# One-core transformer kernel: sums of squares as steps of their own, the latent product regrouped, its copies moved to VectorE, two-strip weight units in one transfer

## The chip, the cores and the metric

The kernel runs on 1 core of one Trainium2 chip. The metric is the device time in microseconds (us), the median of several runs. The engines are called PE (TensorE), DVE (VectorE), ACT (ScalarE), POOL (GpSimd) and SP (SyncE, which here issues nearly all transfers).

## The reference

Two transformer blocks run one after the other on x of 256 tokens by 1024 channels, in float32. The first has a differential attention and a neighbourhood attention beside it, then `x = x + rmsnorm(merged @ w_out)`, then a gated feed-forward part and `x = x + rmsnorm(f)`. The second block begins with a norm and one wide projection, of which these columns matter here:

```
u = rmsnorm_2(h, ln_mix[l])
z = u @ w_in[l]
c_q, c_kv, k_rope, g_q, g_k, g_v, g_lr, g_og, gate_a, gate_b = jnp.split(z, offsets, axis=-1)
...
mix = jax.nn.sigmoid(gate_a) * y_a + jax.nn.sigmoid(gate_b) * y_b
```

`y_a` is a latent attention: c_q (384 columns) and c_kv (256) each get a norm and a further projection (`uq`, `ukv`), k_rope (32) is rotated. `y_b` is a gated linear attention, whose decay comes from g_lr (16). After it come `h = h + mix @ w_out`, a second gated feed-forward part, and a last norm. Everything must come out in float32 accuracy.

## The kernel before, in words

Every large product is made of *strips*: 128 rows of the weight matrix against two token tiles t = 0 and t = 1 of 128 tokens each. To keep accuracy, each float32 operand is split into a high part (rounded by ACT) and a low part (the rest, by DVE), and a strip takes three passes on PE: high by high, high by low, low by high (`product`, line 1019). A strip of 1024 columns is six matmuls of 512 columns per tile. PE has to do all of this, so the other engines have to deliver in time:

- **Weights.** SP loads them into a ring of nine slots (`weights(u)`, line 576), waiting for the slot to be used up by t = 1. ACT splits off the high part (`advance` of the scalar block, line 656), DVE the low part (line 1284 with a gain column, line 1281 without). A planner gives each unit a due time; `advance(ahead_of(i, 2.2))` before each strip does all splits due within 2.2 strips. *Units* are one strip, except in `up5`, `up25` and `gla_qk`, whose narrow strips go two to a slot.
- **Activations.** They are turned (transposed) on PE (`turn`, line 965) into one of four PSUM banks `aux0` to `aux3`, split into high by ACT (`turned_high`, line 664) and low by DVE (line 1303). Before PE writes a bank again it waits for that bank's last reader (`into`).
- **Products** accumulate in `acc`, two banks per token tile. `take(name, t)` empties them; the next product on the same t waits for it (`acc_reader`).

`timeline()` writes one list of steps that every engine walks through in the same order, each doing its own share, and each engine's queue is in order: an instruction that waits holds all that stand behind it. `run(name, sizes, after)` goes through a product in groups of strips, first t = 0 and then t = 1 of each group; `after[t, kt]` are steps put behind strip kt of tile t. So the places that the change touches are:

- **out to up0**: after `take("out", 1)` ACT sums the squares of the result (line 669, tile `silu_tmp`), POOL makes the reciprocal root (lines 1725, 1726), DVE multiplies by the gain (line 1374, `row`) and adds into `x` (line 1381); then `norm_turn("ffn", 1)` turns `x` for the next product. `norm_turn` of the tags `ffn`, `mix2` and `ffn2` also has ACT sum the squares of `x` (`pre_norm`, line 669, tile `row`), and POOL make the root.
- **down to latent**: the same with `down`, `mix2` and `latent`.
- **latent to gla_qk**: `latent` has 688 columns (384 + 304: c_q, c_kv, k_rope, g_lr), in one group of eight strips. Its `take` has ACT copy g_lr out of PSUM (`gate_lr`, line 715) and square c_q and c_kv out of PSUM (line 669, tile `heads`); DVE then copies both to `row` (line 1404), each behind its square, and then k_rope (line 1407). `latent_turn` turns `row` for `uq` and `ukv`, `gate_lr_turn` turns g_lr, and `decay_logits`, two logistic passes on ACT and DVE, and `decay_sums` follow inside `gla_qk`.

## Time and profile before

| | |
|---|---|
| runs | 773.81, 774.9 and 1085.3 us, median 774.9 us |
| the profiled execution's own time | 774.11 us |
| its span | 772.4 us |
| mean granted TensorE clock | 0.999 of full speed (2.4 GHz) |
| PE busy | 760.7 us, 98% of the span |
| DVE, ACT, POOL busy | 473.5, 402.4, 55.8 us |
| moved | 134.34 MB, 174 GB/s in the mean |

The span runs from the first to the last instruction; 1.7 us of the execution's own time lie around it. PE's matmuls overlap and their ends are modelled, so the starts are what to go by: in steady running one 512-column matmul starts 0.23 us after the other.

### The profile page before, as it was taken

What the parts mean: (1) busy time and instruction counts of PE and PEld (TensorE: products, weight loads), DVE (VectorE), ACT (ScalarE), POOL (GpSimd) and SP (SyncE); (2) the same over time, 40 slices, a digit from 0 to 9 for tenths busy, and PEclk for the clock granted to TensorE, in tenths of its full rate; (3) what the DMA queues carried; (4) which work ended last, traced back from release to release, by engine and by line L of the source; (5) the groups of instructions that cost most, each with busy time, mean ns of one, the idle gap of its engine ahead of it and who ended that gap; (6) DMA issues with size and microseconds to landing.
All of it is one profiled execution on the core that took longest, in us unless ns stands there. A gap on an engine that the chain in (4) does not pass through costs nothing.

```text
span 772.4 us, 10412 instructions
## 1 busy us (share of the span) xinstructions
PE 760.7 (98%) x3974; PEld 632.6 (82%) x3974; DVE 473.5 (61%) x705; ACT 402.4 (52%) x599; POOL 55.8 (7%) x130
## 2 busy tenths in 40 slices
PE   8999999999999999999999999999999999999996
PEld 6887878888788888988887787888888888889885
DVE  5576756576855656765357796555765665666632
ACT  5646766444654535544367563666355454444421
POOL 1100100000450000000042000200001000000000
PEclk9999999999999999999999999999999999999999
DMA  8865353555655655654556374342555655564531
GB/s 309 262 190 210 119 191 113 185 161 177 214 170 189 214 161 171 216 165 162 157 173 220 96 227 128 109 162 84 191 170 161 215 180 172 193 205 147 194 136 56
DMA packets 57520, 134.34 MB, mean 174 GB/s; under 512 B 8135, under 2 KB 13438, under 8 KB 57470
## 3 DMA queue, kind: packets, MB, share of 16 engines
q1 hardware_dynamic: 56960, 132.34, 52.7%
q10 hardware_dynamic: 510, 1.33, 0.5%
q8 instruction: 32, 0.52, 0.3%
q14 instruction: 18, 0.15, 0.1%
HBM read 132.60 MB, written 1.05 MB: 173 GB/s over the span
## 4 chain that ended last, share of the span: by engine, by line
PE 95%; ACT 1%; DVE 1%; DMA 1%; issue 1%; POOL 1%; SPq 0%; POOLq 0%; DVEq 0%; ACTq 0%
PE acc L1019 84%; PE aux L965 4%; PE aux L1133 2%; PE aux L1082 1%; PE aux L1112 1%; DMA weights_raw<-in_w_in_dram 1%; PE aux L1205 1%; PE aux L1100 1%; DVE weights_low L1284 0%; PE aux L954 0%; ACT h_high L664 0%; PE aux L1243 0%; ACT row L669 0%; PE aux L1235 0%; ACT silu_tmp L669 0%
## 5 line engine op out<-in xcount | busy, mean ns | idle before, releaser
L1019 PE MATMUL acc<-weights_high,h_high 128*128 128x512 f32 (+2 forms) x752 | 232.7, 389 | 2.6 <-DVE k_rope L1407 1.6
L1284 DVE SCALAR_TENSOR_TENSOR weights_low<-weights_raw,gain_columns,weights_high 128x1024 fp32r<-128x1024 f32 (+3 forms) x189 | 219.2, 1192 | 14.8 <-ACT weights_high L656 13.9
L1019 PE MATMUL acc<-weights_high,h_low 128*128 128x512 f32 (+2 forms) x752 | 225.0, 379 | 0.0
L1019 PE MATMUL acc<-weights_low,h_high 128*128 128x512 f32 (+2 forms) x752 | 224.6, 378 | 0.4 <-DVE weights_low L1284 0.4
L656 ACT ACTIVATE weights_high<-weights_raw,gain_columns 128x1024 fp32r<-128x1024 f32 (+3 forms) x188 | 195.5, 1075 | 25.5 <-DMA weights_raw<-in_w_in_dram 14.7
L1019 PEld LDWEIGHTS acc<-weights_low,h_high 128*128 128x128 f32 x752 | 138.2, 188 | 28.2 <-DVE weights_low L1284 1.3
L1019 PEld LDWEIGHTS acc<-weights_high,h_low 128*128 128x128 f32 x752 | 138.3, 188 | 26.6
L1019 PEld LDWEIGHTS acc<-weights_high,h_high 128*128 128x128 f32 x752 | 133.1, 189 | 28.5 <-issue 4.5
L1281 DVE TENSOR_TENSOR weights_low<-weights_raw,weights_high 128x1024 fp32r<-128x1024 f32 x68 | 80.9, 1220 | 35.9 <-ACT weights_high L656 35.8
L656 ACT ACTIVATE weights_high<-weights_raw 128x1024 fp32r<-128x1024 f32 x68 | 69.4, 1056 | 47.8 <-DMA weights_raw<-in_ffn_w_down_dram 21.8
L1725 POOL TENSOR_SCALAR stats<-stats 128x1 f32<-128x1 f32 (+1 forms) x15 | 8.5, 568 | 625.5 <-ACT row L669 300.8
L1019 PE MATMUL acc<-weights_high,y_high 128*128 128x512 f32 (+1 forms) x148 | 46.6, 396 | 0.0
L1391 DVE SCALAR_TENSOR_TENSOR silu_tmp<-silu_tmp,acc 128x512 f32<-128x512 f32 (+1 forms) x24 | 15.4, 643 | 50.2 <-ACT silu_tmp L712 50.2
L712 ACT ACTIVATE silu_tmp<-acc,stats 128x512 f32<-128x512 f32 (+1 forms) x24 | 15.6, 649 | 58.5 <-PE acc L1019 58.5
L1019 PE MATMUL acc<-weights_high,y_low 128*128 128x512 f32 (+1 forms) x148 | 45.1, 386 | 0.0
L1019 PE MATMUL acc<-weights_low,y_high 128*128 128x512 f32 (+1 forms) x148 | 45.1, 386 | 0.0
L1019 PE MATMUL acc<-weights_high,f_high 128*128 128x512 f32 x112 | 36.1, 396 | 0.0
L1019 PE MATMUL acc<-weights_high,f_low 128*128 128x512 f32 x112 | 36.0, 395 | 0.0
L1019 PE MATMUL acc<-weights_low,f_high 128*128 128x512 f32 x112 | 36.0, 395 | 0.0
L1303 DVE SCALAR_TENSOR_TENSOR y_low<-aux,y_high 128x512 fp32r<-128x512 f32 (+1 forms) x20 | 12.8, 650 | 35.2 <-ACT y_high L664 35.2
L808 ACT ACTIVATE probs<-probs,stats 128x256 f32<-128x256 f32 (+1 forms) x48 | 23.1, 482 | 21.0 <-DVE stats L1515 21.0
L664 ACT ACTIVATE f_high<-aux 128x512 fp32r<-128x512 f32 (+1 forms) x16 | 8.7, 544 | 45.7 <-PE aux L965 45.7
(244 smaller groups left out, 678.0 us busy)
## 6 DMA issues: line engine op xcount, KB each, us to landing
weights_raw<-in_w_in_dram SPq DMA_DIRECT2D x55, 512.0 KB, 5.1
weights_raw<-in_w_down_dram SPq DMA_DIRECT2D x22, 512.0 KB, 4.6
weights_raw<-in_ffn_w_down_dram SPq DMA_DIRECT2D x22, 512.0 KB, 4.5
weights_raw<-in_w_gate_dram SPq DMA_DIRECT2D x40, 256.0 KB, 3.3
weights_raw<-in_w_up_dram SPq DMA_DIRECT2D x40, 256.0 KB, 4.0
weights_raw<-in_ffn_w_gate_dram SPq DMA_DIRECT2D x40, 256.0 KB, 3.4
weights_raw<-in_ffn_w_up_dram SPq DMA_DIRECT2D x40, 256.0 KB, 4.0
weights_raw<-in_w_out_dram SPq DMA_DIRECT2D x16, 512.0 KB, 4.7
```

Source lines behind the costliest of these rows:

```text
L656: nc.scalar.activation(hi[:, u % RING, d:d + w], raw[:, u % RING, d:d + w], ACT.Copy, scale=1.0 if g is None else gcol[:, g:g + 1])\
L664: nc.scalar.activation(dst[0][:, kt0:kt0 + n, t * P:(t + 1) * P], aux[bank][:, 0:n * P].rearrange("p (k s) -> p k s", k=n), ACT.Copy, scal ...
L712: nc.scalar.activation(fe[:, t, 0:w], a0[:, 0:w], ACT.Tanh, scale=stat(("half", (tag, t))))\
L808: j = nc.scalar.activation(T[:, i % 2, hb * 256:hb * 256 + n], T[:, i % 2, hb * 256:hb * 256 + n], ACT.Exp, scale=-1.0, bias=stat(("min", ...
L965: i = nc.tensor.transpose(aux[bank][0:w, n * P:(n + 1) * P], src, ident[:, :])
L1019: i = nc.tensor.matmul(acc[:, 2 * t + b, 0:width], lhs[:, k0, sl], w[:, u % RING, base + d:base + d + width], start=(kt == 0 and n == 0), ...
L1133: m = nc.tensor.matmul(aux[bank][:, d], probs_T[kind][:, i % 2, hb * 256 + kt * P:hb * 256 + (kt + 1) * P], v[:, kt, c], start=(kt == 0), ...
L1281: i = nc.vector.tensor_tensor(lo[:, u % RING, c], raw[:, u % RING, c], hi[:, u % RING, c].bitcast(F32), ALU.subtract)
L1284: i = nc.vector.scalar_tensor_tensor(lo[:, u % RING, c], raw[:, u % RING, c], gcol[:, g:g + 1], hi[:, u % RING, c].bitcast(F32), ALU.mult, ...
L1303: nc.vector.scalar_tensor_tensor(dst[1][:, kt0:kt0 + n, s], aux[bank][:, 0:n * P].rearrange("p (k s) -> p k s", k=n), scale, dst[0][:, kt0 ...
L1391: then(nc.vector.scalar_tensor_tensor(e, e, 1.0, a0[:, 0:w], ALU.add, ALU.mult))
L1725: then(g.tensor_scalar(ms, stat(("ss", key), width), 1.0 / n, EPS, ALU.mult, ALU.add))
```

## The change

Five things are done:

1. The squares of `x` (`pre_norm`) leave `norm_turn` and become steps `stats` of their own, on ACT and POOL: for `up0` and `up20` behind strips (0, 1) and (1, 0), for `latent` behind (0, 1) and (1, 1).
2. On ACT no weight is split at the last two strips of t = 1 of `out` and `down`, so that the squares of the result stand first once PE is done. `norm_turn("mix2", 0)` stands one strip earlier in `down`.
3. `latent` goes in groups of five and three strips. `norm_turn("mix2", 1)` stands behind strip 3 instead of 4. `latent_turn` 0 and 1 move into `gla_qk`, behind (0, 0) and (1, 0); `gate_lr_turn` 0 behind (1, 6), and 1 behind (0, 2).
4. DVE alone empties `latent`: one scaled copy of k_rope and g_lr together (48 columns, tile `k_rope_gate_lr`), then c_q and c_kv to `row`; ACT squares them out of `row` in SBUF instead of PSUM.
5. A unit of two strips comes in one transfer (two in `up5` and `up25`, one for each matrix) instead of two (four).

```diff
@@ timeline @@
     def ffn(up, down, tag, nxt):
-        run(f"{up}0", [4, 4], {(0, 2): [do("norm_turn", tag, 1)], (1, 7): [do("ffn_turn", f"{up}0", 0)]})
+        run(f"{up}0", [4, 4], {(0, 1): [do("stats", tag, 0)], (0, 2): [do("norm_turn", tag, 1)],
+                               (1, 0): [do("stats", tag, 1)], (1, 7): [do("ffn_turn", f"{up}0", 0)]})
...
         if nxt:
-            after[1, KF - 2] = [do("norm_turn", nxt, 0)]
+            after[1, KF - 3] = [do("norm_turn", nxt, 0)]
...
-    run("latent", [8], {(0, 4): [do("norm_turn", "mix2", 1)], (1, 3): [do("latent_turn", 0)],
-                        (1, 5): [do("gate_lr_turn", 0)]})
-    run("gla_qk", [4, 4], {(0, 3): [do("gate_lr_turn", 1)], (1, 2): [do("decay_logits")],
-                           (0, 5): [do("latent_turn", 1)], (1, 7): [do("decay_sums")]})
+    run("latent", [5, 3], {(0, 1): [do("stats", "mix2", 0)], (0, 3): [do("norm_turn", "mix2", 1)],
+                           (1, 1): [do("stats", "mix2", 1)], (1, 6): [do("gate_lr_turn", 0)]})
+    run("gla_qk", [4, 4], {(0, 0): [do("latent_turn", 0)], (0, 2): [do("gate_lr_turn", 1)],
+                           (1, 0): [do("latent_turn", 1)], (1, 2): [do("decay_logits")],
+                           (1, 7): [do("decay_sums")]})
@@ sync: weights(u) @@
+                n = PER.get(name, 1)
+                tile = raw[:, slot, 0:n * width_of(name)].rearrange("p (j w) -> p j w", j=n)
                 for m, kt, c, w, d in loads(u):
-                    src = dram[SC[name][1][m]][0, kt * P:(kt + 1) * P, c:c + w]
-                    sp.dma_start(raw[:, slot, d:d + w], src).then_inc(*tick(f"raw_loaded{slot}", u, 16))
+                    src = dram[SC[name][1][m]][0, kt * P:(kt + n) * P, c:c + w].rearrange("(j p) c -> p j c", p=P)
+                    dst = tile[:, :, d:d + w]
...
@@ scalar: take @@
                 elif name == "latent":
-                    nc.scalar.activation(lr[:, t, :], a1[:, 288:304], ACT.Copy, scale=scaled("mix2", t))\
-                        .then_inc(*tick("act", ("lr", t)))
+                    act.wait_ge(*at("acc_vec", ("latent", t)))
                     junk = ob2[:, t, :].bitcast(BF16)
-                    sum_squares(a0[:, 0:Q_RANK], junk[:, 0:Q_RANK], ("cq", t))
-                    sum_squares(a1[:, 0:KV_RANK], junk[:, Q_RANK:Q_RANK + KV_RANK], ("ckv", t))
+                    for key, c in (("cq", slice(0, Q_RANK)), ("ckv", slice(Q_RANK, Q_RANK + KV_RANK))):
+                        sum_squares(row[:, t, c], junk[:, c], (key, t))
@@ scalar: norm_turn, and the walk through the steps @@
-                    if tag in ("ffn", "mix2", "ffn2"):
-                        pre_norm(tag, t)
...
                 if st[0] == "mm":
+                    if st[1] in ("out", "down") and st[2] == TOKS - 1 and st[3] >= SC[st[1]][2] - 2:
+                        continue
                     advance(ahead_of(i, 0.8 if st[1] == "qk_a" else 2.2))
@@ tensor @@
-                    elif name == "latent":
-                        acc_reader[t] = [("acc_vec", (name, t)), ("act", ("lr", t))]
...
-                    pe.wait_ge(*at("act", ("lr", t)))
-                    turn(("lr", t), 2 + t, [lr[:, t, :]], ("turned_out", ("lr", t)))
+                    pe.wait_ge(*at("vec", ("lr", t)))
+                    turn(("lr", t), 2 + t, [klr[:, t, ROPE:ROPE + 16]], ("turned_out", ("lr", t)))
@@ vector: take @@
                 elif name == "latent":
+                    dve.wait_ge(*at("small2_loaded"))
+                    signal(nc.vector.tensor_scalar(klr[:, t, :], a1[:, KV_RANK:KV_RANK + ROPE + 16],
+                                                   scaled("mix2", t), None, ALU.mult), "vec", ("lr", t))
                     dve.wait_ge(*at("sumsq", ("mix2", t)))
-                    for s, src in ((slice(0, Q_RANK), a0[:, 0:Q_RANK]),
-                                   (slice(Q_RANK, Q_RANK + KV_RANK), a1[:, 0:KV_RANK])):
-                        if s.start:
-                            dve.wait_ge(*at("sumsq", ("ckv", t)))
-                        else:
-                            dve.wait_ge(*at("sumsq", ("cq", t)))
-                        i = nc.vector.tensor_copy(row[:, t, s], src)
...
+                    nc.vector.tensor_copy(row[:, t, 0:Q_RANK], a0[:, 0:Q_RANK])\
+                        .then_inc(*tick("acc_vec", (name, t)))
+                    nc.vector.tensor_copy(row[:, t, Q_RANK:Q_RANK + KV_RANK], a1[:, 0:KV_RANK])\
+                        .then_inc(*tick("acc_vec", (name, t)))
@@ gpsimd: the root for x @@
-                elif kind == "norm_turn":
-                    tag, t, *_ = a
+                elif kind == "stats":
+                    tag, t = a
                     if tag in ("ffn", "mix2", "ffn2"):
                         rstd("sumsq", (tag, t), D)
```

**ACT, from the end of `down` to the turns of the latent rows.** `silu_tmp,stats<-acc` are the squares of the result of `down`, `row,stats<-x` those of `x`, `heads_2` those of c_q and c_kv, `128x688` the splits of the weights of `latent`. Before:

```order
L656 ACTIVATE weights_high<-weights_raw,gain_columns 128x688 x3
L669 ACTIVATE silu_tmp,stats<-acc 128x1024
L656 ACTIVATE weights_high<-weights_raw,gain_columns 128x688 x3
L664 ACTIVATE h_high<-aux0 128x4x128
L664 ACTIVATE h_high<-aux1 128x4x128
L669 ACTIVATE row,stats<-x 128x1024
L656 ACTIVATE weights_high<-weights_raw,gain_columns 128x688
L669 ACTIVATE silu_tmp,stats<-acc 128x1024
L656 ACTIVATE weights_high<-weights_raw,gain_columns 128x688
L664 ACTIVATE h_high<-aux2 128x4x128
L664 ACTIVATE h_high<-aux3 128x4x128
L669 ACTIVATE row,stats<-x 128x1024
```

and now:

```order
L662 ACTIVATE weights_high<-weights_raw,gain_columns 128x688 x2
L675 ACTIVATE silu_tmp,stats<-acc 128x1024
L662 ACTIVATE weights_high<-weights_raw,gain_columns 128x688 x2
L670 ACTIVATE h_high<-aux0 128x4x128
L670 ACTIVATE h_high<-aux1 128x4x128
L675 ACTIVATE silu_tmp,stats<-acc 128x1024
L662 ACTIVATE weights_high<-weights_raw,gain_columns 128x688 x2
L675 ACTIVATE row,stats<-x 128x1024
L662 ACTIVATE weights_high<-weights_raw,gain_columns 128x688 x2
L670 ACTIVATE h_high<-aux2 128x4x128
L670 ACTIVATE h_high<-aux3 128x4x128
```

Two splits have moved from ahead of the first turned halves to behind the second squares of `down`, and `row,stats<-x` has moved behind them; four splits now stand between those squares and the halves of t = 1 (`aux2`, `aux3`).

**DVE, around the two `take`s of `latent`.** `L1404` (now also `L1406`) are the copies of c_q and c_kv to `row`, `128x512` the low parts of the weights of `gla_qk`. Before:

```order
L1404 COPY row<-acc 128x384
L1404 COPY row<-acc 128x256
L1407 TENSOR_SCALAR k_rope<-acc,stats 128x32
L1284 SCALAR_TENSOR_TENSOR weights_low<-weights_raw,gain_columns,weights_high 128x512 x2
L1303 SCALAR_TENSOR_TENSOR y_low<-aux0,y_high 128x4x128
L1303 SCALAR_TENSOR_TENSOR y_low<-aux1,y_high 128x128
L1284 SCALAR_TENSOR_TENSOR weights_low<-weights_raw,gain_columns,weights_high 128x512 x4
L1404 COPY row<-acc 128x384
L1404 COPY row<-acc 128x256
L1407 TENSOR_SCALAR k_rope<-acc,stats 128x32
```

and now:

```order
L1287 SCALAR_TENSOR_TENSOR weights_low<-weights_raw,gain_columns,weights_high 128x688 x2
L1287 SCALAR_TENSOR_TENSOR weights_low<-weights_raw,gain_columns,weights_high 128x512 x4
L1401 TENSOR_SCALAR k_rope_gate_lr<-acc,stats 128x48
L1404 COPY row<-acc 128x384
L1406 COPY row<-acc 128x256
L1287 SCALAR_TENSOR_TENSOR weights_low<-weights_raw,gain_columns,weights_high 128x512 x2
L1401 TENSOR_SCALAR k_rope_gate_lr<-acc,stats 128x48
L1404 COPY row<-acc 128x384
L1406 COPY row<-acc 128x256
```

The copies of t = 1 stood behind four narrow splits and the low parts of the first latent turn; now two narrow splits stand ahead of them, and the low parts come after.

**ACT in `gla_qk`**, from the second squares of c_q and c_kv to the first table load, now:

```order
L675 ACTIVATE heads_2,stats<-row 128x384
L675 ACTIVATE heads_2,stats<-row 128x256
L670 ACTIVATE y_high<-aux0 128x4x128
L670 ACTIVATE y_high<-aux1 128x128
L662 ACTIVATE weights_high<-weights_raw,gain_columns 128x1024
L866 ACTIVATE gate_lr_T<-aux3 16x128
L670 ACTIVATE y_high<-aux2 128x4x128
L670 ACTIVATE y_high<-aux3 128x128
L662 ACTIVATE weights_high<-weights_raw,gain_columns 128x1024
L871 ACT_TABLE_LOAD
```

The turned halves of t = 0 (`y_high`, `aux0` and `aux1`) stood ahead of these squares before; now they stand behind, and the copy of the turned g_lr of t = 1 (`gate_lr_T<-aux3`) behind them and one 1024-column split.

## Rows read from the trace of the kernel before

**Rows 1.** Page, part 1: busy time, share of the span, instructions.

```profile
PE 760.7 (98%) x3974; PEld 632.6 (82%) x3974; DVE 473.5 (61%) x705; ACT 402.4 (52%) x599; POOL 55.8 (7%) x130
```

**Rows 2.** Waits of PE: engine, line, released by: us in total, times, longest.

```profile
PE acc L1019 <- DVE k_rope L1407: 1.6, 1, 1.6
PE aux L965 <- DVE x L1381: 0.7, 2, 0.4
PE acc L1019 <- DVE weights_low L1284: 0.4, 1, 0.4
```

**Rows 3.** Timeline at out to up0: start, us, engine, line, tiles, count [idle before <-releaser].

```profile
195.19 1.03 PE L965 MATMUL aux<-ident,x 128*128 128x128 f32 x8
...
195.98 0.72 PE L1019 MATMUL acc<-weights_high,h_high 128*128 128x512 f32 x2
...
196.80 1.06 ACT L669 ACTIVATE row<-x 128x1024 f32<-128x1024 f32 x1
...
197.84 1.02 ACT L669 ACTIVATE silu_tmp<-acc 128x1024 bf16<-128x1024 f32 x1
...
198.83 2.20 ACT L656 ACTIVATE weights_high<-weights_raw,gain_columns 128x1024 fp32r<-128x1024 f32 x2
...
201.23 1.41 DVE L1381 SCALAR_TENSOR_TENSOR x<-row,stats,x 128x512 f32<-128x512 f32 x2 [0.93 <-POOL stats L1726]
...
202.04 1.32 PE L965 MATMUL aux<-ident,x 128*128 128x128 f32 x8 [0.31 <-DVE x L1381]
```

**Rows 4.** Timeline at down to latent.

```profile
385.82 0.87 ACT L656 ACTIVATE weights_high<-weights_raw,gain_columns 128x688 fp32r<-128x688 f32 x1 [1.29 <-DMA weights_raw<-in_w_in_dram]
...
386.27 0.63 PE L1019 MATMUL acc<-weights_low,f_high 128*128 128x512 f32 x2
386.60 1.06 ACT L664 ACTIVATE h_high<-aux 128x512 fp32r<-128x512 f32 x2
...
387.27 0.55 PE L1019 MATMUL acc<-weights_high,h_high 128*128 128x384 f32 x2 [0.37 <-issue]
...
388.59 0.87 ACT L656 ACTIVATE weights_high<-weights_raw,gain_columns 128x688 fp32r<-128x688 f32 x1
...
389.36 1.02 ACT L669 ACTIVATE silu_tmp<-acc 128x1024 bf16<-128x1024 f32 x1
...
390.25 0.47 PE L1019 MATMUL acc<-weights_high,h_high 128*128 128x384 f32 x2
...
392.67 1.32 PE L965 MATMUL aux<-ident,x 128*128 128x128 f32 x8 [0.39 <-DVE x L1381]
```

**Rows 5.** Timeline at latent to gla_qk.

```profile
401.81 2.73 ACT L656 ACTIVATE weights_high<-weights_raw,gain_columns 128x512 fp32r<-128x512 f32 x4 [3.87 <-DMA weights_raw<-in_w_in_dram]
...
407.68 0.27 PE L965 MATMUL aux<-ident,gate_lr 128*16 128x128 f32 x1
...
408.50 0.88 DVE L1404 COPY row<-acc 128x384 f32<-128x384 f32 x2
...
409.30 0.24 DVE L1407 TENSOR_SCALAR k_rope<-acc,stats 128x32 f32<-128x32 f32 x1
...
409.59 0.50 PE L1019 MATMUL acc<-weights_high,h_high 128*128 128x512 f32 x1 [1.65 <-DVE k_rope L1407]
...
409.94 0.40 PE L1019 MATMUL acc<-weights_high,h_low 128*128 128x512 f32 x1
...
410.18 0.40 PE L1019 MATMUL acc<-weights_low,h_high 128*128 128x512 f32 x1
...
417.12 0.69 DVE L1584 SCALAR_TENSOR_TENSOR log_decay<-log_decay,level_decay 128x512 f32<-128x512 f32 x1 [2.65 <-ACT level_decay L871]
...
419.82 1.05 PE L1180 MATMUL aux<-sum_up_to,log_decay 128*128 128x128 f32 x8
```

**Rows 6.** DMA issues: tensor, queue, count, KB each, median us to landing.

```profile
weights_raw<-in_w_in_dram SPq DMA_DIRECT2D x55, 512.0 KB, 5.1
...
gates<-in_rpb_dram SPq DMA_DIRECT2D x2, 438.0 KB, 12.1
```

More of the change, by code:

```diff
@@ L143, in loads @@
     out = []
-    for k, base, _ in strips(u):
-        for m, c, w, d in sorted(SC[name][3], key=lambda p: p[3]):
-            if out and out[-1][0] == m and out[-1][1] == k and out[-1][2] + out[-1][3] == c:
-                out[-1][3] += w
-            else:
-                out.append([m, k, c, w, base + d])
+    for m, c, w, d in sorted(SC[name][3], key=lambda p: p[3]):
+        if out and out[-1][0] == m and out[-1][2] + out[-1][3] == c:
+            out[-1][3] += w
+        else:
+            out.append([m, kt, c, w, d])
     return out
@@ L407, in program @@
             sil = sb("silu_og", [P, TOKS, 512], F32, s)
-            lr = sb("gate_lr", [P, TOKS, 16], F32, s)
+            klr = sb("k_rope_gate_lr", [P, TOKS, ROPE + 16], F32, s)
+            kr = klr[:, :, 0:ROPE].rearrange("p t (a d) -> p t a d", a=2)
             lrT = sb("gate_lr_T", [16, SEQ], F32, s)
@@ L411, in program @@
             vm = sb("v_latent", [P, TOKS, 512], F32, s)
-            kr = sb("k_rope", [P, TOKS, 2, 16], F32, s)
             rt = sb("rope_tmp", [P, 2, MLA_H, 2, 16], F32, s)
@@ L682, in take @@
                 a0, a1 = acc[:, 2 * t, :], acc[:, 2 * t + 1, :]
-                if name not in ("branch_a", "branch_b", "gla_o", "mla_o", "out2", "down2"):
+                if name not in ("branch_a", "branch_b", "gla_o", "mla_o", "out2", "down2", "latent"):
                     act.wait_ge(*at("mm_done", (name, t)))
@@ L1151, in step @@
                     t, = a
-                    pe.wait_ge(*at("vec", ("latent", t)))
+                    pe.wait_ge(*at("acc_vec", ("latent", t)))
                     turn(("latent", t, 0), 2 * t, slices(row[:, t, 0:512], 4), ("turned_low", ("latent", t, 0)))
@@ L1436, in take @@
                         ALU.mult), "acc_vec", (name, t))
-                    k = kr[:, t, :, :].rearrange("p a b -> p (a b)").rearrange("p (o d) -> p o d", o=1)\
+                    k = klr[:, t, 0:ROPE].rearrange("p (o d) -> p o d", o=1)\
                         .to_broadcast([P, MLA_H, ROPE])
```

10 lines of the change are left out of this document (4 added, 6 removed).

## The prediction

> **What bounds the kernel now.** I read the busy times first: PE is busy for 760.7 of 772.4 us [rows 1], at a granted clock of 0.999, so only what PE waits can be won here: 772.4 - 760.7 = 11.7 us in all. The reader is to see that the large busy shares of DVE and ACT say nothing of a bound, since neither is full. Second, the waits of PE [rows 2]: the longest inside the program is 1.6 us for DVE's k_rope, then come two for `x` and one for low weights, 2.7 us together. Third, the timelines of the three passages, for who holds whom.
>
> At out to up0, ACT squares `x` of t = 0 at 196.80 and only then, at 197.84, the result of t = 1; `x` then also waited 0.93 us for POOL, and PE waited 0.31 us for `x` at 202.04 [rows 3]. The eight transposes there span 1.32 us, where eight that find everything ready span 1.03 [rows 3]: 0.29 us more is lost between their halves. (The next product starts 195.98 - 195.19 = 0.79 us after the first of them.)
>
> At down to latent, ACT waited for a weight transfer with the turned halves queued behind it (split at 385.82, halves at 386.60), and PE stood 0.37 us until 387.27; later it waited 0.39 us for `x`, and its transposes again span 1.32 us [rows 4].
>
> At latent to gla_qk, PE's last transpose began at 407.68, and its next product only at 409.59, when DVE had done k_rope, the last of three copies that stood behind ACT's squares [rows 5].
>
> One correction of size: the profile counts idle time from a matmul's modelled end, 0.40 us after its start, but matmuls follow each other in 410.18 - 409.94 = 0.24 us [rows 5]. So each gap costs about 0.16 us more than its idle figure, and the first matmul after the long one cost 409.94 - 409.59 = 0.35 instead of 0.24 us.
>
> **The change part by part.**
>
> *Out to up0.* ACT's squares of the result of t = 1 no longer stand behind those of `x` (1.06 us, [rows 3]) or behind a split; POOL has no root of `x` ahead of them either. DVE's `x` came at 201.23; it can come about 0.9 us sooner, since the 0.93 us for POOL go, and PE's wait with its split transposes goes: 0.31 + 0.16 + 0.29 = 0.76 us. What is late next are the halves of t = 1 behind ACT's work after PE's end of `out`: squares 1.02, two splits 2.2, squares of `x` 1.06, one split 1.1 [rows 3], together 5.4 us, against three strips, the transposes and a fourth strip: 4 x 6 x 0.23 + 0.79 = 6.3 us. They fit, by 0.4 us, with the first half's own 0.53 us added (1.06 for two, [rows 4]).
>
> *Down to latent, start.* The turned halves get one strip more of cover (1.4 us) and no split that waits for a transfer stands directly ahead. The gap of 0.37 + 0.16 = 0.53 us goes. `down` ends on PE at about 386.9 in either kernel (386.27 + 0.63, [rows 4]).
>
> *Down to latent, t = 1.* The squares of the result now start at 386.9 instead of 389.36, 2.4 us sooner; `x` with them. PE needs it 0.94 us sooner than before, after four strips instead of five (one strip is (390.25 - 387.27) / 3 = 0.99 us by the rows, first strip included [rows 4]; I take 0.95). So 0.39 + 0.16 + 0.29 = 0.84 us go. But something comes in its place. ACT idles until PE is done, because no split is allowed in between, and then has squares 1.02, four splits at 389.36 - 388.59 = 0.77 each, 3.1, and the squares of `x`, 1.06, ahead of the halves of t = 1 [rows 4], as its order now shows: 5.1 us, the first half ready at 386.9 + 5.1 + 0.5 = 392.6. PE arrives at strip (1, 0) after four strips, transposes and a fifth: 386.7 + 4.75 + 0.79 = 392.25. That is a new wait of 0.4 us; its bounds are 0 (each action is 0.07 us shorter) and 1.2 (the transfers' wait of 1.29 us at 385.82 comes back there). I take 0.4.
>
> *Latent to gla_qk.* The copies of DVE no longer wait for squares, k_rope comes first, and PE waits for c_kv's copy. With the groups of five and three, PE does three more strips of the other tile and several turns between; behind the end of `latent` it has strips (0, 0) to (0, 3) of `gla_qk` and the turns, 4 x 0.69 + 0.6 = 3.3 us, before it needs the bank of t = 1. DVE needs 0.24 and 0.88 for its copies, and has at most two narrow splits of 2.73 / 4 = 0.7 us ahead [rows 5]: 2.5 us. The gap goes: 1.65 + 0.16 + 0.11 = 1.9 us. Slots of `latent`'s first five strips also come free three strips (2.8 us) earlier, so the 3.87 us that ACT waited for weights at 401.81 [rows 5] move ahead of PE's need, and the 0.4 us for weights_low [rows 2] with them; I count 0.1.
>
> *What is queued behind the new waits.* ACT now waits for DVE's copies before it squares. Behind that wait stand the halves of the latent turn, a 1024-column split and the copy of the turned g_lr, and PE's second turn of `row` for t = 1 goes into the very bank (`aux3`) that this copy has to free. From the end of `latent`: DVE 1.2, squares 0.8 to 0.9 (as wide as DVE's copies of 0.88), halves 0.8, split 1.1, copy 0.25, 4.2 us; PE gets there after 3.3 + 0.7 + 0.4 = 4.4 us. I cost it at nothing; each us of lateness costs one, bounds 0 and 1. The decay chain has room: its result came at 417.12 + 0.69 = 417.8, PE wanted it at 419.82 [rows 5], 2.0 us of slack; a latent turn of 0.5 us has left the stretch between, so 1.5 are left.
>
> The Trainium skill, "VectorE: DVE Perf Modes", section on the TRN2 errata, speaks against squaring out of `row`: ScalarE pays a fixed 224 cycles from SBUF and 172 from PSUM, 0.04 us more for each of four squares by its figure. The trace agrees on 1024 columns (1.06 us from `x` against 1.02 from acc, [rows 3]). It changes nothing in the sum.
>
> *Transfers.* Twelve units take one issue or two fewer each. SP is never what PE waits for [rows 2], so I count 0. A whole unit of 512 KB lands in 5.1 us in the median [rows 6]; the planner's lead covers it. Bounds: nothing to a wait, priced as a rival below.
>
> *Sum.* 0.76 + 0.53 + 0.84 + 1.9 + 0.1 = 4.1 us go, 0.4 come: 3.7 us. The profiled execution took 774.1 us (its span and 1.7 us around it), so 770.4; the runs' median is 774.9, 0.8 above, which is within what runs differ, and I put 770.5.
>
> **The rivals.**
>
> *The waits shift (0.27).* Everything works, but ACT's tighter queue gives part back: 1.2 us at latent (1, 0), 0.7 at the turn into `aux3`. For it: both margins are 0.4 us or less. Against: ACT waited 1.29 and 3.87 us for transfers around here [rows 4, 5] and has room in total. 770.5 + 0.8 + 0.7 = 772.0 us.
>
> *The change doesn't remove the wait (0.08).* PE still waits in `gla_qk` because DVE, not ACT's squares, was late: low splits still stand ahead of its copies, and each of them waits for ACT. Then 1.9 us stay, and the new waits of the rival above take most of the rest: 773.9 us, no change.
>
> *Slower (0.03): a late transfer in front of the copies.* DVE's order now has four narrow low splits of `gla_qk` ahead of the first latent copies. The second unit's load starts when strip (1, 0) is used, about 393.6, and PE wants the turned g_lr at 402.1. If the one transfer lands as late as the slowest of [rows 6], 12.1 us, that is 405.7; two high splits, the last low one and the 48-column copy make 2.3 us more, so PE waits to 408.0: 5.9 us, 776.4 us. It costs PE from a landing time of 6.2 us on, and from 9.9 us on the kernel is slower than before. Against: 5.1 in the median.
>
> The Trainium skill, "Perfetto Trace Analysis", part on the Tensor Engine Instruction, says that ACT, DVE and GPSIMD are strict FIFO. The trace agrees: halves ready to be done stood behind a 1.29 us wait for weights [rows 4]. Both rivals that cost time live on this.
>
> **How the numbers follow.** Forecast 0.60, shift 0.27, wait stays 0.08, slower 0.03, and 0.02 for something better than forecast. The range goes from 768.8 (no new wait, 0.4, and 1.3 for gaps that the profile doesn't name and runs that differ) to 774.6 (shift and unchanged included). A measurement of this kernel tells about 2%, 15.5 us, from no change. PE's whole idle time is 11.7 us, so faster by more than that is all but excluded: 0.01. The slower rival is far from 15.5 us as well: 0.02. Within 2%: 0.97.
>
> **What would show it right or wrong.** Right: PE's row for DVE's copies of `latent` is gone from its waits; the `x` rows too; eight transposes take 0.79 us in both passages; PE busy stays near 760.7 and the span falls by what its idle time falls. A wait of PE for `h_high` at the first strip of t = 1 in `latent`, of about 0.4 us, would show the new wait. Wrong: a row of PE for k_rope_gate_lr or `row`, for gate_lr_T, or a DVE wait for ACT's weights_high of over 2 us ahead of the latent copies.

## The result, and the profile after

| | before | after |
|---|---|---|
| median | 774.5 us (4 runs) | 770.25 us (4 runs, 770.12 to 770.56) |
| the profiled execution's own time | 774.11 us | 770.12 us |
| its span | 772.4 us | 768.4 us |
| PE busy | 760.7 us | 758.9 us |
| span less PE busy | 11.7 us | 9.5 us |

The ratio of after to before is 0.9948, 95% interval 0.9937 to 0.996. By the measure of 2% that is no change; by the intervals it is 0.5% faster, and 770.5 us had been forecast. (One execution of before took 1085.3 us, and one of the last experiment 1085.68; they stand in the medians and not in the ratios.)

Page of after, part 1, the row that answers to [rows 1]:

```profile
PE 758.9 (99%) x3974; PEld 632.6 (82%) x3974; DVE 473.6 (62%) x705; ACT 401.9 (52%) x597; POOL 55.4 (7%) x130
```

The instructions of PE are the same in number, and DVE and ACT are busy for as long as before within 0.5 us (ACT has two instructions less, its copies of g_lr): the 4.0 us are waiting time. PE's busy time fell too, by 1.8 us: work that PE waited for is booked longer (0.50 us for the matmul at 409.59 and 0.40 for others in [rows 5], 1.32 and 1.03 us for eight transposes in [rows 3]), so busy time holds part of the gaps.

Waits of PE in after (columns as in [rows 2]; 1.7 us for `ident` at the start of the program, the same in both kernels, are left out):

```profile
PE acc L1024 <- ACT weights_high L650: 0.5, 1, 0.5
PE acc L1024 <- ACT weights_high L653: 0.4, 1, 0.4
PE acc L1024 <- DVE weights_low L1287: 0.4, 1, 0.4
PE acc L1024 <- ACT h_high L670: 0.2, 1, 0.2
```

The rows for k_rope and for `x` of [rows 2] are gone. Two rows are new. The 0.4 us for weights_high of line 653 lies at 7.58 us, at the start of the program, where the change does nothing; of it and its neighbours the kernels show now one and now the other. The 0.2 us for `h_high` is the new wait of the passages. The 0.4 us for weights_low is not in the three passages either: the timeline has it at 8.90 us, and before at 8.97.

Timeline of after at out to up0 (columns as in [rows 3]):

```profile
197.54 1.02 ACT L675 ACTIVATE silu_tmp<-acc 128x1024 bf16<-128x1024 f32 x1 [0.75 <-PE acc L1024]
...
198.81 0.19 POOL L1724 TENSOR_SCALAR stats<-stats 128x1 f32<-128x1 f32 x1 [5.53 <-ACT silu_tmp L675]
...
200.04 1.41 DVE L1384 SCALAR_TENSOR_TENSOR x<-row,stats,x 128x512 f32<-128x512 f32 x2
...
201.44 1.03 PE L970 MATMUL aux<-ident,x 128*128 128x128 f32 x8
...
202.23 0.72 PE L1024 MATMUL acc<-weights_high,h_high 128*128 128x512 f32 x2
```

ACT is idle when PE ends `out` and squares the result at once; DVE's `x` starts at 200.04 without a wait for POOL, 1.2 us sooner than in [rows 3]. The eight transposes span 1.03 us instead of 1.32 and do not wait, and the next product follows 202.23 - 201.44 = 0.79 us after the first of them.

Most of this comes from POOL, not from ACT. Timeline of before:

```profile
198.11 0.88 POOL L1725 TENSOR_SCALAR stats<-stats 128x1 f32<-128x1 f32 x1 [4.69 <-ACT row L669]
...
200.27 0.19 POOL L1725 TENSOR_SCALAR stats<-stats 128x1 f32<-128x1 f32 x1
```

There the root for `x` of t = 0, begun at 198.11, stood ahead of the root of the result, which POOL began at 200.27, 1.4 us after ACT's squares had ended. Now POOL begins it at 198.81. From the first transposes of the passage on (195.19 and 195.06), ACT's squares are only 0.17 us sooner, POOL's root 1.33 us.

Timeline of after at down to latent:

```profile
385.81 0.47 PE L1024 MATMUL acc<-weights_high,h_high 128*128 128x384 f32 x2
...
386.00 1.02 ACT L675 ACTIVATE silu_tmp<-acc 128x1024 bf16<-128x1024 f32 x1 [2.13 <-PE acc L1024]
...
387.02 1.62 ACT L662 ACTIVATE weights_high<-weights_raw,gain_columns 128x688 fp32r<-128x688 f32 x2
...
389.55 1.09 PE L970 MATMUL aux<-ident,x 128*128 128x128 f32 x8
389.58 1.62 ACT L662 ACTIVATE weights_high<-weights_raw,gain_columns 128x688 fp32r<-128x688 f32 x2
...
391.10 1.05 ACT L670 ACTIVATE h_high<-aux 128x512 fp32r<-128x512 f32 x2
...
391.82 0.55 PE L1024 MATMUL acc<-weights_high,h_high 128*128 128x384 f32 x2 [0.24 <-ACT h_high L670]
```

`latent` starts straight behind `down`, where [rows 4] had 0.37 us at 387.27. ACT's 2.13 us of idle time ahead of 386.00 is the place where the change forbids splits. The squares and four splits then stand ahead of the halves at 391.10, and PE waits 0.24 us for these at 391.82.

Timeline of after at latent to gla_qk:

```profile
397.72 1.34 ACT L662 ACTIVATE weights_high<-weights_raw,gain_columns 128x512 fp32r<-128x512 f32 x2 [3.29 <-DMA weights_raw<-in_w_in_dram]
...
398.48 1.41 DVE L1287 SCALAR_TENSOR_TENSOR weights_low<-weights_raw,gain_columns,weights_high 128x512 fp32r<-128x512 f32 x2 [2.46 <-ACT weights_high L662]
...
399.81 0.26 DVE L1401 TENSOR_SCALAR k_rope_gate_lr<-acc,stats 128x48 f32<-128x48 f32 x1
...
401.27 0.27 PE L970 MATMUL aux<-ident,k_rope_gate_lr 128*16 128x128 f32 x1
...
402.54 0.27 DVE L1401 TENSOR_SCALAR k_rope_gate_lr<-acc,stats 128x48 f32<-128x48 f32 x1 [0.35 <-PE acc L1024]
...
406.23 0.25 ACT L866 ACTIVATE gate_lr_T<-aux 16x128 f32<-16x128 f32 x1
...
406.49 0.71 PE L970 MATMUL aux<-ident,row 128*128 128x128 f32 x5
...
413.81 0.69 DVE L1583 SCALAR_TENSOR_TENSOR log_decay<-log_decay,level_decay 128x512 f32<-128x512 f32 x1 [2.64 <-ACT level_decay L874]
...
415.85 1.05 PE L1183 MATMUL aux<-sum_up_to,log_decay 128*128 128x128 f32 x8
```

`gla_qk` starts at 402.33 without a wait. DVE stood idle (0.35 us) until `latent` of t = 1 ended, and copied at once; in [rows 5] its last copy came 1.6 us after PE's last transpose. Ahead of its copies of t = 0 DVE does wait 2.46 us for ACT's splits (398.48), but the turn that needs them comes only at 401.27, 1.2 us after the first copy has ended.

In before, what held DVE's copies of t = 1 was DVE's own queue. Timeline of before:

```profile
405.05 0.89 DVE L1303 SCALAR_TENSOR_TENSOR y_low<-aux,y_high 128x512 fp32r<-128x512 f32 x2 [4.97 <-ACT y_high L664]
405.85 2.73 DVE L1284 SCALAR_TENSOR_TENSOR weights_low<-weights_raw,gain_columns,weights_high 128x512 fp32r<-128x512 f32 x4
```

DVE stood 4.97 us for the halves of the first latent turn, which came late because ACT had waited 3.87 us for weights ([rows 5], 401.81); then it did four low parts, and the copies followed at 408.50 without a pause. ACT's squares of t = 1 had ended at 408.05 by then and held nothing.

The decay sums start at 415.85 instead of 419.82, 3.97 us sooner, and the span is 4.0 us shorter: all of the gain lies ahead of this point.

### The profile page after: what moved, and what is told of

Read it like the earlier page. It is cut to its first block, busy times and chain, and to the rows that moved or that the text cites. A ratio compares the mean times of both kernels' runs of the same rounds, so it can differ in the third digit from the quotient of the medians.

```text
span 768.4 us, 10385 instructions
## 1 busy us (share of the span) xinstructions
PE 758.9 (99%) x3974; PEld 632.6 (82%) x3974; DVE 473.6 (62%) x705; ACT 401.9 (52%) x597; POOL 55.4 (7%) x130
## 3 DMA queue, kind: packets, MB, share of 16 engines
q10 hardware_dynamic: 510, 1.33, 0.5%
## 4 chain that ended last, share of the span: by engine, by line
PE 97%; ACT 1%; DMA 1%; DVE 0%; issue 0%; POOL 0%; SPq 0%; ACTq 0%; POOLq 0%
PE acc L1024 86%; PE aux L970 4%; PE aux L1136 2%; PE aux L1085 1%; PE aux L1115 1%; PE aux L1208 1%; PE aux L1103 1%; DMA weights_raw<-in_w_in_dram 1%; ACT weights_high L662 0%; PE aux L1246 0%; PE aux L1238 0%; DVE weights_low L1287 0%; PE aux L1223 0%; PE aux L1171 0%; ACT row L675 0%
```

## The experiments

Each kernel is the changed one with one edit, or with two where the text says so. Of each, PE's start of `latent` and of the decay sums give the length of the stretch between them (30.04 us in after, 32.55 before). Starts of a passage differ by up to 0.5 us among kernels that are alike up to there (`latent` starts at 385.78 to 386.29), so lengths are compared and not the clock times.

**Two transfers for two strips.** Part 5 undone.

```diff
-                    src = dram[SC[name][1][m]][0, kt * P:(kt + n) * P, c:c + w].rearrange("(j p) c -> p j c", p=P)
...
+                for j in range(n):
+                    for m, kt, c, w, d in loads(u):
+                        src = dram[SC[name][1][m]][0, (kt + j) * P:(kt + j + 1) * P, c:c + w]
+                        sp.dma_start(tile[:, j, d:d + w], src).then_inc(*tick(f"raw_loaded{slot}", u, 16))
```

> The changed kernel, but a unit of two strips comes in two (four) transfers again. My theory: SP is never what PE waits for, so this part is worth nothing: 770.3 us, within 0.3, and PE waits of the changed kernel unchanged. Rival: the single transfer brings the second unit of gla_qk earlier and is part of the 4.2 us: 770.8 us or more, and ACT waits longer for DMA at its 512-column splits than 3.29 us.

Measured: 770.2 us (769.92 to 770.33), ratio to before 0.9942, interval 0.993 to 0.9954. The transfers are worth nothing.

**The passage from out as before.** The squares go back to their turns, `norm_turn("ffn", t)` and `stats` together (for t = 0 in `out`, a line that isn't shown), and the splits are no longer left out in `out`.

```diff
+        if tag == "ffn":
+            run(f"{up}0", [4, 4], {(0, 2): [do("norm_turn", tag, 1), do("stats", tag, 1)],
+                                   (1, 7): [do("ffn_turn", f"{up}0", 0)]})
...
-                    if st[1] in ("out", "down") and st[2] == TOKS - 1 and st[3] >= SC[st[1]][2] - 2:
+                    if st[1] == "down" and st[2] == TOKS - 1 and st[3] >= SC[st[1]][2] - 2:
```

> The changed kernel, but out to up0 as before: the squares of x back in the turns of tag ffn, and splits on ACT allowed at the last strips of out. My theory, the term of the prediction: 0.76 us comes back, 771.0 us, PE waits 0.3 us for x and its transposes of t = 1 span 1.32 us again. Rival: only the 0.31 us of counted idle time was to be won, 770.6 us.

Measured: 771.04 us (770.93 to 771.4), ratio 0.9954, 0.9941 to 0.9967; 0.79 us over after. Timeline of this kernel at the place:

```profile
201.49 1.41 DVE L1388 SCALAR_TENSOR_TENSOR x<-row,stats,x 128x512 f32<-128x512 f32 x2 [0.92 <-POOL stats L1729]
...
202.30 0.99 PE L974 MATMUL aux<-ident,x 128*128 128x128 f32 x5 [0.31 <-DVE x L1388]
```

Both waits of [rows 3] are back (0.92 for 0.93 us, and 0.31). This part was sized at 0.76. That it is the place of the squares, and not that of the splits, the run with part 2 undone shows (below): there the passage is as long as in after, 7.17 us from the first transposes to the product behind the second.

**One group.** `latent` in one group of eight with the turns at their old places, DVE's new copies kept: order against copies.

```diff
-    run("latent", [5, 3], {(0, 1): [do("stats", "mix2", 0)], (0, 3): [do("norm_turn", "mix2", 1)],
-                           (1, 1): [do("stats", "mix2", 1)], (1, 6): [do("gate_lr_turn", 0)]})
...
+    run("latent", [8], {(0, 1): [do("stats", "mix2", 0)], (0, 4): [do("norm_turn", "mix2", 1)],
+                        (0, 6): [do("stats", "mix2", 1)], (1, 3): [do("latent_turn", 0)],
+                        (1, 5): [do("gate_lr_turn", 0)]})
```

> The changed kernel, but latent in one group of eight and all turns where they stood before; DVE alone still copies. Two theories of the 2.5 us won between the start of latent and decay_sums. A, the copies: DVE no longer waits for ACT's squares, that is all; then this kernel keeps the gain, 770.3 to 770.8 us, no wait of PE at the first strip of t = 1 in gla_qk. B, the order: DVE's copies stood behind four low splits, which stood behind ACT's splits, which waited 3.87 us for weights whose slots came free late; then DVE is as late as before and PE waits 1 to 1.7 us for DVE's second copy of latent: 772.0 us.

Measured: 772.27 us (771.66 to 773.94, 12 runs), ratio 0.9975, 0.9967 to 0.9983; 2.0 us over after. Timeline of DVE and PE in this kernel:

```profile
402.52 0.89 DVE L1306 SCALAR_TENSOR_TENSOR y_low<-aux,y_high 128x512 fp32r<-128x512 f32 x2 [5.58 <-ACT y_high L670]
403.32 2.73 DVE L1287 SCALAR_TENSOR_TENSOR weights_low<-weights_raw,gain_columns,weights_high 128x512 fp32r<-128x512 f32 x4
...
405.97 0.27 DVE L1401 TENSOR_SCALAR k_rope_gate_lr<-acc,stats 128x48 f32<-128x48 f32 x1
...
406.29 0.28 PE L970 MATMUL aux<-ident,k_rope_gate_lr 128*16 128x128 f32 x1 [0.86 <-DVE k_rope_gate_lr L1401]
...
407.08 0.49 PE L1024 MATMUL acc<-weights_high,h_high 128*128 128x512 f32 x1 [0.52 <-DVE row L1406]
```

DVE's copies no longer wait for ACT's squares, and yet PE waits for them, 1.38 us in two waits: they stand behind the low halves of the first latent turn, for which DVE stood 5.58 us, and four narrow low parts. So theory B holds: freeing the copies from ACT isn't enough; what stands ahead of them on DVE decides.

**Old copies.** The new groups, but ACT copies g_lr and squares out of PSUM, and DVE's copies wait for the squares, as before.

```diff
-                    act.wait_ge(*at("acc_vec", ("latent", t)))
+                    nc.scalar.activation(klr[:, t, ROPE:ROPE + 16], a1[:, 288:304], ACT.Copy,
+                                         scale=scaled("mix2", t)).then_inc(*tick("act", ("lr", t)))
...
+                            dve.wait_ge(*at("sumsq", ("ckv", t)))
+                        else:
+                            dve.wait_ge(*at("sumsq", ("cq", t)))
+                        i = nc.vector.tensor_copy(row[:, t, s], src)
```

> The changed kernel with the groups of five and three and the new places of the turns, but the copies of before: ACT copies g_lr and squares out of PSUM, DVE copies each part behind its square and k_rope last. A, the copies matter: PE waits again about 1.5 us in gla_qk, 772.0 us. B, the order matters: the chain gets about 0.5 us longer in each take but there are now 3.3 us of PE work between: 770.3 to 770.9 us, at most a wait of 0.3 us for the turned g_lr or for row.

Measured: 770.98 us (770.59 to 771.82), ratio 0.9954, 0.9942 to 0.9966; 0.73 us over after. Timeline of this kernel:

```profile
400.37 1.34 ACT L662 ACTIVATE weights_high<-weights_raw,gain_columns 128x512 fp32r<-128x512 f32 x2 [1.11 <-DMA weights_raw<-in_w_in_dram]
...
402.82 0.89 DVE L1410 COPY row<-acc 128x384 f32<-128x384 f32 x2 [2.72 <-ACT heads L675]
...
403.92 0.50 PE L1025 MATMUL acc<-weights_high,h_high 128*128 128x512 f32 x1 [0.77 <-DVE k_rope_gate_lr L1413]
```

A transfer holds ACT's splits, these hold the squares, these hold DVE's copies of t = 0, and PE waits. The transfer isn't later than in after (400.37 is 14.21 us behind the start of `latent`; there the same splits come 14.20 us behind it): what differs is that DVE copied at 399.81 in after, ahead of these splits, and here has to wait for the squares behind them. This execution took 771.82 us, the longest of the five, so the trace shows the way and the median the size.

**Old groups and old copies together.** The two edits above at once; of the change there remain the passages out to up0 and down to latent, and the transfers.

> The changed kernel with both the one group of eight (and old places of the turns) and the old copies; out to up0, the start of latent and the transfers stay changed. Completes the four combinations: both new 770.25, old order alone 772.27, old copies alone 770.98. If the two parts act on the same wait, the order sets it and this kernel takes 772.3 to 772.7 us. If they add up, 772.27 + 0.73 = 773.0 us or more.

Measured: 773.17 us (771.9 to 774.22, 12 runs), ratio 0.9982, 0.9972 to 0.9991. The median lies between two clusters, and the granted clock tells them apart: six executions at 0.998 or 0.999 took 771.9 to 772.82 (median 772.25), six at 0.996 took 773.52 to 774.22 (773.88). In the experiment with one group nine at 0.998 or 0.999 had a median of 772.19, and three at 0.996 took 773.49 to 773.94. The median of all twelve lies where the rival had put it (773.0 or more). At the same clock the two kernels are equal, so with the old groups the old copies add nothing but, it may be, more executions at the lower clock (six of twelve against three, too few to tell): the two stand for one wait. That comparison by clock was made afterwards; what the clock does is in the last section.

By medians at the higher clock: old groups and copies 772.25, new groups alone 770.98, new copies alone 772.19, both 770.25. The order brings 1.3 us by itself, the copies 0.1 by themselves and 0.7 on top of the order.

**ACT splits at the last strips.** Part 2 undone: the two lines with `continue` are taken out.

> The changed kernel, but ACT may split weights at the last two strips of out and down again. Theory: at down two splits stand ahead of the squares again, the second waits for its transfer until about 385, so the squares start about 0.8 us later and x with them; PE waits 0.3 to 0.5 us for x and its transposes split: 770.9 us. Rival: ACT was idle for 2.1 us there, the splits fit, and leaving them out is worth nothing or costs: 770.2 us or less, since fewer splits then stand ahead of the halves of t = 1.

Measured: 770.09 us (770.05 to 770.31), ratio 0.994, 0.9927 to 0.9952. The loss that was expected didn't come. Timeline of ACT in this kernel:

```profile
384.11 0.87 ACT L662 ACTIVATE weights_high<-weights_raw,gain_columns 128x688 fp32r<-128x688 f32 x1
386.36 1.02 ACT L675 ACTIVATE silu_tmp<-acc 128x1024 bf16<-128x1024 f32 x1 [1.38 <-PE acc L1022]
```

One split falls into time in which ACT stood idle anyway (1.38 us of idle time are left of 2.13), and the next comes behind the squares, at 387.37. Nothing is held up, one split less stands ahead of the halves of t = 1, and the new wait is gone. In the changed kernel part 2 brings nothing, at `out` neither.

**Splits left out at the last strip only.** The `- 2` of part 2 becomes `- 1`.

> The changed kernel, but ACT leaves out splits only at the last strip of out and down, not at the last two. One split of latent then falls into the 2.13 us that ACT idles before the squares. Theory: 0.8 us less of work ahead of the halves of t = 1, the wait of 0.24 us goes: 769.9 us. Rival: that split's weights land too late and hold the squares: 770.5 us or more.

Measured: 770.08 us (769.65 to 770.69), ratio 0.994, 0.9926 to 0.9954; start of `latent` to sums 29.88 us, 0.16 less than in after. The wait goes, as was expected, but with half of the gain that was expected (769.9).

**Squares of `x` behind the turn.** `stats("mix2", 0)` stands behind `norm_turn("mix2", 1)` instead of behind strip (0, 1).

```diff
-    run("latent", [5, 3], {(0, 1): [do("stats", "mix2", 0)], (0, 3): [do("norm_turn", "mix2", 1)],
+    run("latent", [5, 3], {(0, 3): [do("norm_turn", "mix2", 1), do("stats", "mix2", 0)],
```

> The changed kernel, but the squares of x of t = 0 for latent stand behind the turn of t = 1, so ACT reaches the halves of t = 1 1.04 us sooner. Theory: the wait of 0.24 us of PE for h_high goes with its restart, 0.3 to 0.4 us: 769.9 us. Rival: something else is late right there (the low part of strip 4, or the low halves), and the time stays 770.2 us.

Measured: 770.14 us (769.88 to 770.57), ratio 0.994, 0.9928 to 0.9953. The wait for `h_high` is gone from PE's waits, but the stretch to the sums is only 0.18 us shorter. Timeline of PE and DVE in this kernel:

```profile
389.81 1.77 DVE L1287 SCALAR_TENSOR_TENSOR weights_low<-weights_raw,gain_columns,weights_high 128x688 fp32r<-128x688 f32 x2
...
391.50 1.28 DVE L1306 SCALAR_TENSOR_TENSOR h_low<-aux,h_high 128x512 fp32r<-128x512 f32 x2
...
391.70 0.47 PE L1024 MATMUL acc<-weights_low,h_high 128*128 128x384 f32 x2
...
392.25 0.58 PE L1024 MATMUL acc<-weights_high,h_low 128*128 128x384 f32 x2
```

Passes of this product start every 0.31 us; the one with `h_low` starts 0.55 us after its forerunner. No idle figure stands beside it. ACT has the high halves ready at 391.25, but DVE begins the low ones at 391.50, straight behind two low parts of weights. The rival of the expectation holds: DVE's own queue now ends last, and the same 0.54 to 0.55 us stand there in the other kernels without the wait.

**Both together.** Part 2 undone and the squares behind the turn, to beat both kernels.

> A version meant to beat both: the changed kernel with splits allowed at all strips of out and down, and the squares of x of t = 0 for latent behind the turn of t = 1. Each alone took away the wait of 0.24 us at the first strip of t = 1 in latent and came to 770.09 and 770.14 us; both act on the same wait, so together again 770.0 to 770.2 us. If they added up it would be 769.9 us or less.

Measured: 770.05 us (769.71 to 770.24), ratio 0.9942, 0.9929 to 0.9954: the lowest median of all, by 0.2 us under after, which is within what runs differ. What the new wait gives back is 0.16 to 0.18 us of the stretch to the sums, whichever way it is removed (in all four kernels it is 29.86 to 29.88 us).

**ACT 1 us later.** An unused sum of squares over 1024 columns of `x` behind the latent squares of t = 1.

```diff
+                    if t:
+                        nc.scalar.activation(spare[:, :], x[:, 0, :], ACT.Square, accum_out=stat("spare")).then_inc(
+                            *tick("sumsq", "spare"))
```

> The changed kernel, with one more square of 1024 columns on ACT (about 1.0 us) behind the squares of c_q and c_kv of t = 1, thus ahead of the copy of the turned g_lr that frees aux3. Its result isn't used. The prediction's margin there: PE's turn into aux3 comes about 0.4 us after the copy in the changed kernel's trace. Theory: what exceeds 0.4 us is paid, 0.6 us plus 0.1 to 0.2 for the gap, 770.9 to 771.1 us, and a wait of PE for gate_lr_T. Rival: ACT has slack there and nothing is paid, 770.3 us, or everything behind it on ACT slips and more than 1 us is paid.

Measured: 770.97 us (770.88 to 771.88), ratio 0.9953, 0.994 to 0.9965; 0.72 us over after. Timeline of its profiled execution (the one of 771.88):

```profile
408.61 0.33 PE L974 MATMUL aux<-ident,row 128*128 128x128 f32 x1 [1.04 <-ACT gate_lr_T L870]
```

The wait stands where the prediction had put it, at the fifth transpose into `aux3`. In after that transpose comes at about 406.9 and the copy ends at 406.48: 0.4 us of slack, so 1 us more of ACT should cost 0.6 and a gap, and by the median it does. The wait of 1.04 us is longer than that because this execution is the longest of the five: a pair of narrow splits on ACT had waited for its transfer until 401.15, 14.86 us behind the start of `latent` instead of 14.20.

**One and two transfers of 512 KB ahead of the second unit of `gla_qk`.** SP loads an unused tile and waits for it before it issues the unit; with `range(2)` twice.

```diff
+                if u == FIRST["gla_qk"] + 1:
+                    for _ in range(1):
+                        sp.dma_start(spare[:, :], dram["x"][0, 0:P, :]).then_inc(*tick("spare_loaded", None, 16))
+                        sp.wait_ge(*last_of("spare_loaded"))
```

> The changed kernel, but SP loads 512 KB that nobody uses, and waits for them, before it loads the second unit of gla_qk; so that unit lands 4 to 4.5 us later. The slower rival of the prediction, priced: DVE's low splits of that unit stand ahead of its copies of latent. In the changed kernel's trace the turn of g_lr of t = 0 comes 1.2 us after its copy, so what exceeds 1.2 us is paid: about 3 us, 773.2 us, with a wait of PE for k_rope_gate_lr. If instead the time stays below 771 us, the transfer has more slack than that and the rival was never near.

> The same with two such transfers one after the other, 8 to 9 us later. By the rival's rule about 7 us are paid: 777 us, slower than the kernel before (774.5). If the cost is not proportional (under 775 us), the ring's other slots make up for it.

Measured: with one, 772.6 us (771.73 to 773.75, 10 runs), ratio 0.9978, 0.9968 to 0.9987. With two, 777.34 us (from 776.4, 8 runs; 777.05 without the one of 1085.68), ratio 1.0038, 1.0025 to 1.0051: slower than before. Timeline with one, then with two:

```profile
400.73 2.66 ACT L667 ACTIVATE weights_high<-weights_raw,gain_columns 128x512 fp32r<-128x512 f32 x4 [6.14 <-DMA weights_raw<-in_w_in_dram]
...
403.14 0.28 PE L975 MATMUL aux<-ident,k_rope_gate_lr 128*16 128x128 f32 x1 [1.55 <-DVE k_rope_gate_lr L1406]
```

```profile
403.70 1.33 ACT L667 ACTIVATE weights_high<-weights_raw,gain_columns 128x512 fp32r<-128x512 f32 x2 [9.15 <-DMA weights_raw<-in_w_in_dram]
...
405.79 0.26 DVE L1406 TENSOR_SCALAR k_rope_gate_lr<-acc,stats 128x48 f32<-128x48 f32 x1
...
406.11 0.38 PE L975 MATMUL aux<-ident,k_rope_gate_lr 128*16 128x128 f32 x1 [4.53 <-DVE k_rope_gate_lr L1406]
```

The slot came free at 393.2 in both (SP's first extra load). The unit was there 7.5 and 10.5 us later, in after 397.72 - 393.07 = 4.65 us later. So one transfer ahead delays it by 2.9 us, not by the 4 to 4.5 expected, and costs 2.35 us, 0.6 less than expected. Two delay it by 5.9 us, not by 8 to 9, and cost 6.8 to 7.1 us: that this is the 7 us expected is luck. The wait is 4.53 us, and another 1.9 us come from the lower clock behind it (last section), which the expectation didn't have. PE's waits put the point from which a late landing costs at 7.5 - 1.55 = 10.5 - 4.53 = 6.0 us. The way through ACT's and DVE's queues is as the prediction's slower rival has it.

## Why the prediction was right

The time (770.5 against 770.25) held, and so did the mechanism in the main: PE's waits in the three passages go, because what it waits for no longer stands behind other work. The steps one by one:

- **Out to up0**, 0.76 us. From after's start at 195.06 instead of 195.19 to the product behind the second turn at 202.23 instead of 203.11: 0.75 us. Undone alone: 0.79. The prediction named both ACT's order and POOL's; POOL's is what the traces show as the larger.
- **Start of latent**, 0.53 us. 387.27 to 385.81 is 1.46, of which 0.88 came from out to up0 with its earlier start: 0.58. No run undoes this part alone. Part 2 isn't its cause (below); that the turn one strip earlier is, is likely and not shown.
- **From there to the decay sums**, 0.84 + 1.9 + 0.1 - 0.4 = 2.44 us. Measured 32.55 - 30.04 = 2.51. The 0.84 is a little low: in the kernel with old groups and old copies, which keeps the eight strips and the old turn here, the way from the start of `latent` to the product behind the turn takes 391.47 - 386.00 = 5.47 us, before 393.74 - 387.27 = 6.47: 1.0 us. The 0.1 for weights_low rested on a misreading: that wait is at the start of the program and stayed. The new wait was placed rightly (strip (1, 0), for `h_high`) and sized at 0.4; PE idled 0.24, and with the 0.16 us that each gap costs beyond its idle figure that is 0.4. But its removal brought only 0.16 to 0.18, because the pause for `h_low` comes up under it: what a gap costs isn't what its removal gives where a second chain ends a moment later.
- **The cause of the 1.9 us.** The prediction named both the copies' freedom from ACT and the regrouping, and gave no split. Its reading that in before the copies of t = 1 "stood behind ACT's squares" is wrong: they stood behind low halves and low parts on DVE. The runs give the split: the order is the larger share (1.3 us by itself), and the copies pay only with it.
- **The turn into `aux3`**, costed at nothing with a slack of 4.4 - 4.2 = 0.2 us: 0.4 us measured, and a later ACT cost what this slack says.
- **The decay chain**, 1.5 us of slack left: 415.85 - (413.81 + 0.69) = 1.35.
- **Transfers**, 0: shown by undoing them.
- **Part 2 of the change** was taken to be part of what frees ACT; it isn't needed. That "no split that waits for a transfer stands directly ahead" of the turned halves holds without it as well: in the run with part 2 undone ACT waits for PE's turn itself, and its split comes behind the halves, at 384.11. In the sum that made no difference.
- **The signs.** The rows of PE went and the new wait came as written. "PE busy stays near 760.7" did not hold: it fell by 1.8 us, since busy time books part of each gap. Eight transposes take 0.79 us to the next product at `up0` and 390.40 - 389.55 = 0.85 at `latent`. And one sign of being wrong appeared, a wait of DVE of over 2 us for ACT's weights_high ahead of the latent copies (2.46 us at 398.48). It was badly chosen: the copies have 1.2 us of slack behind it, so by itself it costs nothing.

The rivals. *The waits shift*: a shift of 0.24 us, not 1.5. *The change doesn't remove the wait*, because low parts stand ahead of the copies: not so with the new groups, but just so with one group (2.0 us over after). *Slower*: costs from 6.0 us of landing time on, where 6.2 was written. With 10.5 us of landing time its own arithmetic gives 10.5 - 6.2 = 4.3 us over the forecast, 774.8 us; 777.34 was measured, since it left out what the clock does behind such a wait, 1.9 us. In the changed kernel the unit landed after 4.65 us.

The Trainium skill, "Perfetto Trace Analysis", part on the Tensor Engine Instruction, has ACT and DVE as strict FIFO. The extra loads show it here: ACT's splits at 403.70 and DVE's copy behind them moved by 5.98 us each against after (from 397.72 and from 399.81, to 403.70 and 405.79), though the copy needs no weights.

The Trainium skill, "VectorE: DVE Perf Modes", section on the TRN2 errata, gives ScalarE a dearer start from SBUF than from PSUM. The trace agrees. Timeline of after, then of the experiment with old copies:

```profile
401.25 0.51 ACT L675 ACTIVATE heads<-row 128x384 bf16<-128x384 f32 x1
```

```profile
404.13 0.46 ACT L675 ACTIVATE heads<-acc 128x384 bf16<-128x384 f32 x1
```

The same squares take 0.05 us more from `row`. It changes nothing: ACT has the room.

## What to carry to other kernels

When an engine that is always busy waits for a copy, look at what stands ahead of the copy in its own queue before freeing it from another engine: here the copies freed from ACT brought 0.1 us alone and 0.7 us once the order was changed. Look at every engine of the chain, the small ones too: at out to up0 it was POOL's queue. Compute for each moved step how much time lies between its result and its need (0.4, 1.35 and 1.2 us of slack here), and test the smallest by making the supplier late on purpose. And when a short wait goes, expect the next chain right behind it: a wait of 0.24 us, which cost 0.4, was worth 0.16 to 0.18.

## What the runs showed of the hardware beside that

A wait of PE can cost more than its length, for the granted clock can fall behind it. Windows of 2 us of PE in the profiled execution (774.22 us) of the kernel with old groups and old copies: stretch, length, PE busy (instructions), granted clock, DMA share, GB/s:

```profile
406.00:408.00 2.00, 0.54 (x3) 1.00 1.04 399
408.00:410.00 2.00, 1.82 (x5) 0.57 0.30 110
410.00:412.00 2.00, 2.00 (x6) 0.58 0.00 0
```

and its timeline:

```profile
405.23 0.50 PE L1025 MATMUL acc<-weights_low,h_high 128*128 128x512 f32 x1 [0.73 <-DVE weights_low L1290]
...
408.18 0.73 PE L1025 MATMUL acc<-weights_high,h_high 128*128 128x512 f32 x1 [1.63 <-DVE k_rope_gate_lr L1413]
...
411.69 0.40 PE L1025 MATMUL acc<-weights_low,h_high 128*128 128x512 f32 x1
```

PE stood 0.73 and then 1.63 us, and the eight matmuls from 408.18 to 411.69 start 0.42 to 0.52 us apart instead of 0.23: the engine runs at the lower of its two levels, 1.2 instead of 2.4 GHz. They take 3.51 us instead of 8 x 0.23 = 1.84: 1.67 us more, as much as lies between the clusters of this kernel (773.88 - 772.25 = 1.63). The Trainium skill, "TensorE: Matmul & The Clock Gate", section "Wait — 56ns, not 53.3ns?", has 426.7 ns from one 512-column matmul to the next at the lower level, and the trace agrees; at the higher one it has 215.7 ns, where these stand 0.23 us apart.

With two transfers ahead the clock of the profiled execution is 0.88 and then 0.50 in the two windows from 402 to 406 us, in which PE stands, and 0.50 up to 410. From the turn at 406.11 to the second matmul behind the turn of `row` the work takes 410.59 - 406.11 = 4.48 us, in after 403.82 - 401.27 = 2.55: 1.9 us more. The mean clock of all eight executions is 0.996 or less. After itself and the kernels with no long wait in these passages (two transfers for two strips, part 2 undone, one strip, squares later, both together) show 0.997 or more in 29 of 29 executions; before showed 0.996 in 7 of 49 beside the experiments, with about 776 us against 774.2. A wait of 1.65 us doesn't always do it: in before's own profiled execution the windows from 406 to 414 us all show 1.00. That the seven are the same event is likely, since before has the 1.65 us wait at that place, but none of them was profiled: it isn't shown. If it is so, the change also takes away this rare loss, which the medians don't count.
